# A fused two-block layer on one core: soft attention with the first map's scores two tiles ahead, another queue order on VectorE and ScalarE, and operand splits in three pieces

## The chip, the cores and the metric

One core of a Trainium2 chip runs the whole program in one launch. The metric is the device time in microseconds; lower is better. Of the kernel before, three runs gave 3892.44, 3895.23 and 3902.70 us.

## What is computed

Two transformer-like blocks over 1024 tokens of width 1024 in fp32: a block with a convolution branch, differential attention and a mixture of experts, then a block with four mixers and a feed-forward part. The change touches two attentions with a softmax over all earlier tokens. The first block's is differential: each of 4 heads has two maps of 64 channels, and the second map's weights are taken off the first's:

```python
s = einsum("bqhcd,bkhcd->bhcqk", qi, k) * scale      # c: the two maps
s = where(key_pos <= q_pos, s, -inf)
p = softmax(s, axis=-1)
a = p[:, :, 0] - lam * p[:, :, 1]
return einsum("bhqk,bkhe->bqhe", a, v)
```

The second block's (`_fox`) has 4 heads of 64 channels and a decay added to the scores: `s = q k + c_q - c_k`, masked, softmax, times v.

## The kernel before

`soft_attention` (L663) serves both. The **paired** call (tag `da`, from `first_block`, L2776) works on 4 pairs of maps, one head each; the **unpaired** call (tag `fx`, from `mixers`, L2842) on 2 pairs, two heads each. A *unit* u is a pair i and a tile t of 128 queries: t runs from 0 to 7 (NT = 8), and since attention is causal, a unit has t+1 tiles of 128 keys. x is 0 or 1, the map in the pair. All engines go through the units in one list, each with a queue order of its own, written out by hand; counting semaphores tie them.

**Operands.** fp32 scores come from fp32r matmuls, so q and k are split into a rounded part and a remainder. `round_off` (ScalarE, L782) writes the rounded part: three copies for a map (L785, L786, L789), four in the unpaired call (L788 too). `remainders` (VectorE, L829) writes the differences, two for a map (L833, L834), once `hi_made` says that the copies are there. `lo_made` frees the scores. The split is made in two pieces of columns, 0 to 256 and 256 to 1024, each waited for at t=0 and t=2. There is one buffer for all pairs, so the split of the next pair waits until the last scores of this one are done. In the unpaired call POOL also moves two rows of decay for each map by DMA (L714), and the scores of t=0 wait for both.

**A unit.** `scores` (TensorE, L724) fills two PSUM banks for each map (0 and 1, 2 and 3) by L732 and L733, and L734 adds the mask; it waits for the exponential of the unit before on the same map, which frees the banks. `peaks` (VectorE, L840) takes the row maxima. `exps` (ScalarE, L796) takes exponentials and their sums. `combine` (VectorE, L846 to L851) takes the sums' reciprocals and, in the paired call, adds the second map's weights to the first's by L851. `turn_weights` (TensorE, L747) transposes the weights in chunks of up to four tiles, which alternate between banks 4 and 5: chunk c waits until chunk c-2 has been kept. The paired call turns one map (1 or 2 chunks a unit), the unpaired call two (2 chunks, 4 from t=4 on). `keep_turned` (ScalarE, L806) copies them out of PSUM. `weigh` (TensorE, L759) multiplies by the values, t+1 matmuls for a map, of 128 columns in the paired and 64 in the unpaired call, each with two records in the trace; it has banks 6 and 7. `finish` (VectorE, L858) scales the result.

**Queue order before,** in the iteration of unit u (within a pair):

```python
TensorE: scores(u+1, 0), scores(u+1, 1), turn_weights(u), weigh(u-1)
ScalarE: exps(u+1, 0), keep_turned(u), exps(u+1, 1)
VectorE: peaks(u+1, 0), combine(u), peaks(u+1, 1), finish(u-1)
```

In the iteration of t=7 TensorE issues the next pair's scores behind weighing, ScalarE the first piece ahead of the keeping copy and the second between the exponentials of the next t=0, and VectorE the differences likewise.

Of the kernel before, what the change touches and what calls it, by code (L numbers as in the profile page):

```python
# [662 lines left out]
def soft_attention(K, tag, q_tiles, k_tiles, values, v_col, dv, o, o_col, paired, exps_room, turned_room, decay=None):  # L663
# [7 lines left out]
    pieces = ((0, 2 * P), (2 * P, S))  # L671
# [9 lines left out]
    with ExitStack() as scope, nc.Block() as block:  # L681
# [20 lines left out]

        def exps_of(u, x, n):
            return exps_room[u % 2][x][:, 0:n]

        if decay is not None:
            @block.gpsimd
            def _(pool):
                pool.wait_ge(filled, 1)
                for i in range(pairs):  # L710
                    for x in range(2):
                        if i:
                            pool.wait_ge(scored, 2 * (NT * i - 1) + x + 1)
                        pool.dma_start(k2[(1 - x) * HD:(1 - x) * HD + 2, x, :], decay[2 * i + x]).then_inc(decay_landed, 16)  # L714

        @block.tensor
        def _(pe):
            mm = nc.tensor.matmul

            def scores(u, x):  # L720
                i, t = units[u]
                if t in (0, 2):
                    pe.wait_ge(lo_made, 4 * i + 2 * (t > 0) + x + 1)
                if t == 0 and decay is not None:  # L724
                    pe.wait_ge(decay_landed, 32 * i + 32)
                if u:
                    pe.wait_ge(exped, 2 * (u - 1) + x + 1)
                n, queries = (t + 1) * P, slice(t * P, (t + 1) * P)
                bank = score_bank(x, n)
                for b in range(0, n, HALF):  # L730
                    keys = slice(b, min(b + HALF, n))
                    mm(bank[:, keys], q1[:, x, queries], k1[:, x, keys], start=True, stop=False)  # L732
                    mm(bank[:, keys], q2[:, x, queries], k2[:, x, keys], start=False, stop=(keys.stop < n))  # L733
                mm(bank[:, n - P:n], K.ident_r[:], K.causal_r[:], start=False, stop=True).then_inc(scored, 1)  # L734
# [28 lines left out]
            for x in range(2):  # L763
                scores(0, x)
            for u, (i, t) in enumerate(units):
                ahead = u + 1 if u + 1 < len(units) else None
                if t < NT - 1:
                    scores(ahead, 0)
                    scores(ahead, 1)
                turn_weights(u)  # L770
                if u:
                    weigh(u - 1)
                if t == NT - 1 and ahead:
                    scores(ahead, 0)
                    scores(ahead, 1)
# [3 lines left out]
        def _(act):  # L779
            def round_off(i, piece):  # L780
                cols = slice(*pieces[piece])
                for x in range(2):  # L782
                    if i:
                        act.wait_ge(scored, 2 * (NT * i - 1) + x + 1)
                    nc.scalar.activation(k1[own(x), x, cols], k_tiles[own(x), i, cols], ACT.Copy)  # L785
                    nc.scalar.activation(q1[own(x), x, cols], q_tiles[own(x), i, cols], ACT.Copy)  # L786
                    if decay is not None:
                        nc.scalar.activation(q2[own(x), x, cols], q_tiles[own(x), i, cols], ACT.Copy)  # L788
                    nc.scalar.activation(k1[other(x), x, cols], k_tiles[own(x), i, cols], ACT.Copy).then_inc(hi_made, 1)  # L789
# [19 lines left out]
            for piece in range(2):  # L809
                round_off(0, piece)  # L810
            for x in range(2):
                exps(0, x)
            for u, (i, t) in enumerate(units):
                if t < NT - 1:
                    exps(u + 1, 0)
                    keep_turned(u)
                    exps(u + 1, 1)
                    continue
                if i + 1 < pairs:
                    round_off(i + 1, 0)  # L820
                keep_turned(u)
                if i + 1 < pairs:
                    exps(u + 1, 0)
                    round_off(i + 1, 1)
                    exps(u + 1, 1)

        @block.vector
        def _(dve):
            def remainders(i, piece):  # L829
                cols = slice(*pieces[piece])  # L830
                for x in range(2):
                    dve.wait_ge(hi_made, 4 * i + 2 * piece + x + 1)
                    nc.vector.tensor_tensor(k2[own(x), x, cols], k_tiles[own(x), i, cols], k1[own(x), x, cols].bitcast(F32), ALU.subtract)  # L833
                    nc.vector.tensor_tensor(q1[other(x), x, cols], q_tiles[own(x), i, cols], q1[own(x), x, cols].bitcast(F32),  # L834
                                            ALU.subtract).then_inc(lo_made, 1)
# [35 lines left out]
            for piece in range(2):  # L871
                remainders(0, piece)
            for x in range(2):
                peaks(0, x)
            for u, (i, t) in enumerate(units):
                if t < NT - 1:
                    peaks(u + 1, 0)
                    combine(u)
                    peaks(u + 1, 1)
                    if u:  # L880
                        finish(u - 1)
                    continue
                combine(u)
                if i + 1 < pairs:
                    remainders(i + 1, 0)
                finish(u - 1)
                if i + 1 < pairs:
                    peaks(u + 1, 0)
                    remainders(i + 1, 1)
                    peaks(u + 1, 1)  # L890
# [2021 lines left out]
```

## Time and profile before

| | us |
|---|---|
| median of three runs | 3895.23 |
| the profiled execution, its own time | 3911.31 |
| its span, first to last instruction | 3909.3 |
| mean granted TensorE clock | 0.863 |
| TensorE, VectorE, ScalarE, GpSimd busy | 3215.3, 1489.7, 1110.4, 243.3 |
| paired call | some 374 to 566 |
| unpaired call | some 2205 to 2320 |

All times in the rows are counted from the start of the span. An engine's queue is strictly in order, so an instruction that waits holds up all behind it. "Idle before" is the time in which the engine did nothing ahead of the instruction, with the one that released it. The clock is the share of full speed that TensorE was granted.

### The profile page before, as it was taken

The page shows a single profiled execution, that of the slowest core. Times are in us where ns is not written, and L with a number is a line of the kernel's source. Part 1 is how long each engine was busy: PE and PEld are TensorE (multiplying, and loading weights), DVE is VectorE, ACT ScalarE, POOL GpSimd, SP SyncE. Part 2 cuts the span into 40 slices and gives each one's busy share as a digit, 9 for nine tenths or more (in the row PEclk, how much of TensorE's full clock was granted, in tenths as well). Part 3 has the DMA queues.
Part 4 walks back from the last instruction along what each step waited for, and adds up shares of the span by engine and source line. Part 5 has one row for each costly group of instructions (what it writes and reads, how often), then busy time and mean ns, then how long its engine had stood idle before and what let it go on. Part 6 is the DMA issues. An engine that isn't in the chain of part 4 may idle for free. (4 is left out here: it accounts for less than half of the span.)

```text
span 3909.3 us, 40094 instructions
## 1 busy us (share of the span) xinstructions
PE 3215.3 (82%) x14307; PEld 2421.1 (62%) x14307; DVE 1489.7 (38%) x1914; ACT 1110.4 (28%) x1677; POOL 243.3 (6%) x279
## 2 busy tenths in 40 slices
PE   4994659999389999993999478962796789999998
PEld 3882556667345555552788366741794668888786
DVE  2996561113323333334000422368334443333334
ACT  3123541112233333334121543330011432222232
POOL 0220000000100000001221000100000000000000
PEclk8996889999699999996999775565577989999999
DMA  2115002102389999983211101100000311111122
GB/s 77 38 44 172 1 1 66 47 16 86 115 313 343 335 344 334 341 323 140 59 43 31 60 11 28 27 3 11 12 0 14 121 43 54 43 53 43 39 95 75
DMA packets 267644, 391.13 MB, mean 100 GB/s; under 512 B 34001, under 2 KB 150792, under 8 KB 267560
## 3 DMA queue, kind: packets, MB, share of 16 engines
q1 hardware_dynamic: 246344, 339.06, 25.7%
q0 software_dynamic: 9392, 29.99, 2.3%
q10 hardware_dynamic: 11824, 21.00, 1.4%
q8 instruction: 48, 0.79, 0.1%
q14 instruction: 36, 0.29, 0.0%
HBM read 334.33 MB, written 55.68 MB: 100 GB/s over the span
## 5 line engine op out<-in xcount | busy, mean ns | idle before, releaser
L1743 PE MATMUL banks<-h_hi,u_w_hi 128*128 128x512 f32 x704 | 274.8, 390 | 10.6 <-DVE u_w_lo L1777 10.6
L1744 PE MATMUL banks<-h_lo,u_w_hi 128*128 128x512 f32 x704 | 274.6, 390 | 0.0
L1745 PE MATMUL banks<-h_hi,u_w_lo 128*128 128x512 f32 x704 | 274.4, 390 | 0.0
L1381 PE MATMUL banks<-e_wg,e_xT 128*128 128x512 f32 x512 | 227.6, 598 | 1.2 <-ACT e_xT L1411 1.2
L1381 PE MATMUL banks<-e_wu,e_xT 128*128 128x512 f32 x512 | 224.9, 592 | 0.0
L485 DVE SCALAR_TENSOR_TENSOR conv<-x_first,vectors,conv 128x1024 f32<-128x1024 f32 x120 | 183.8, 1531 | 9.0
L1451 DVE TENSOR_TENSOR e_wd_lo<-e_wd,e_wd_hi 128x1024 fp32r<-128x1024 f32 x128 | 148.2, 1220 | 95.7 <-ACT e_wd_hi L1423 95.7
L1381 PEld LDWEIGHTS banks<-e_wu,e_xT 128*128 128x128 f32 x512 | 97.3, 190 | 122.5 <-issue 122.5
L1381 PEld LDWEIGHTS banks<-e_wg,e_xT 128*128 128x128 f32 x512 | 98.0, 192 | 112.9 <-issue 110.5
L1743 PEld LDWEIGHTS banks<-h_hi,u_w_hi 128*128 128x128 f32 x704 | 132.6, 188 | 38.6 <-issue 11.0
L1423 ACT ACTIVATE e_wd_hi<-e_wd 128x1024 fp32r<-128x1024 f32 x128 | 124.7, 1045 | 110.4 <-DVE e_y L1461 110.2
L1744 PEld LDWEIGHTS banks<-h_lo,u_w_hi 128*128 128x128 f32 x704 | 132.6, 188 | 27.6
L1745 PEld LDWEIGHTS banks<-h_hi,u_w_lo 128*128 128x128 f32 x704 | 132.6, 188 | 27.5
L1597 PE MATMUL banks<-fd_w_hi,fd_s_hi 128*128 128x512 f32 x352 | 138.2, 393 | 8.8 <-DVE fd_s_lo L1656 8.6
L377 PE MATMUL banks<-h_hi,z_w_hi 128*128 128x512 f32 x320 | 127.7, 399 | 12.6 <-POOL z_w_lo L440 12.6
L1598 PE MATMUL banks<-fd_w_lo,fd_s_hi 128*128 128x512 f32 x352 | 137.6, 391 | 0.0
L1599 PE MATMUL banks<-fd_w_hi,fd_s_lo 128*128 128x512 f32 x352 | 137.5, 391 | 0.0
L328 PE MATMUL banks<-consts,n_xn 128*128 128x128 f32 x192 | 43.5, 406 | 104.4 <-ACT n_xn L277 104.3
L378 PE MATMUL banks<-h_lo,z_w_hi 128*128 128x512 f32 x320 | 127.4, 398 | 0.0
L379 PE MATMUL banks<-h_hi,z_w_lo 128*128 128x512 f32 x320 | 127.3, 398 | 0.0
L940 PE MATMUL banks<-h_hi,m_w_hi 128*128 128x512 f32 x256 | 105.2, 411 | 7.4 <-DVE m_w_lo L978 7.4
L1396 PE MATMUL banks<-e_wd_hi,e_midT_hi 128*128 128x512 f32 x256 | 103.1, 403 | 7.0 <-ACT e_midT_hi L1428 7.0
(519 smaller groups left out, 6747.1 us busy)
## 6 DMA issues: line engine op xcount, KB each, us to landing
e_wg<-in_w_gate_e_dram SPq DMA_DIRECT2D x32, 2048.0 KB, 8.9
e_wu<-in_w_up_e_dram SPq DMA_DIRECT2D x32, 2048.0 KB, 16.3
e_wd<-in_w_down_e_dram SPq DMA_DIRECT2D x32, 2048.0 KB, 14.1
yT<-in_ffn_w_up_dram SPq DMA_DIRECT2D x44, 512.0 KB, 3.9
expert_results<-nothing SPq DMA_DIRECT2D x1, 16384.0 KB, 50.1
expert_results<-e_y ACTq DMA_DIRECT2D x32, 512.0 KB, 7.1
fd_w<-in_ffn_w_down_dram SPq DMA_DIRECT2D x44, 256.0 KB, 2.6
z_w<-in_w_in_dram SPq DMA_DIRECT2D x19, 512.0 KB, 3.8
```

Of the source, the lines that this page charges most:

```text
L377: mm(bank, w_hi[:, b, cols], h_hi[:, k, tokens], start=(k == 0), stop=False)
L378: mm(bank, w_hi[:, b, cols], h_lo[:, k, tokens], start=False, stop=False)
L379: last = mm(bank, w_lo[:, b, cols], h_hi[:, k, tokens], start=False, stop=(k == KT - 1))
L485: nc.vector.scalar_tensor_tensor(conv[:, c, :], y[:, c, j:j + S], tap(j), conv[:, c, :], ALU.mult, ALU.add)
L1381: mm = nc.tensor.matmul(bank, xT[:, b, k, :], w[:, b, k, :], start=(k == 0), stop=(k == KT - 1))
L1451: nc.vector.tensor_tensor(wd_lo[:, k, :], wd[:, b, k, :], wd_hi[:, k, :].bitcast(F32), ALU.subtract) \
L1597: nc.tensor.matmul(K.ps[:, t, :], s_hi[:, b, tokens], w_hi[:, b, :], start=first, stop=False)
L1598: nc.tensor.matmul(K.ps[:, t, :], s_hi[:, b, tokens], w_lo[:, b, :], start=False, stop=False)
L1599: mm = nc.tensor.matmul(K.ps[:, t, :], s_lo[:, b, tokens], w_hi[:, b, :], start=False, stop=last)
L1743: nc.tensor.matmul(bank, w_hi[:, up, k, :], h_hi[:, k, tokens], start=(k == 0), stop=False)
L1744: nc.tensor.matmul(bank, w_hi[:, up, k, :], h_lo[:, k, tokens], start=False, stop=False)
L1745: mm = nc.tensor.matmul(bank, w_lo[:, up, k, :], h_hi[:, k, tokens], start=False, stop=(k == KT - 1))
```

## The change

The scores of map 0 go two units ahead, those of map 1 one ahead: `scores(u+2, 0)` stands between turning and weighing, `scores(u+1, 1)` ahead of turning. VectorE has `combine(u)` first, then `peaks(u+1, 1)`, `peaks(u+2, 0)` and `finish(u-1)`. ScalarE has both exponentials of u+1 and then the keeping copy of u. The split is made in three pieces (0 to 256, 256 to 512, 512 to 1024; waited for at t=0, 2 and 4): the first in the iteration of t=6 of the pair before, the second in that of t=7, the third in those of t=0 (map 0) and t=1 (map 1) of the pair itself. No operation is added or removed but for the extra piece. The same order holds in both calls.

```diff
--- before.py
+++ after.py
@@ -668,7 +668,8 @@
     pairs = q_tiles.shape[1]
     units = [(i, t) for i in range(pairs) for t in range(NT)]
     outs = 1 if paired else 2
-    pieces = ((0, 2 * P), (2 * P, S))
+    pieces = ((0, 2 * P), (2 * P, HALF), (HALF, S))
+    starts = {0: 0, 2: 1, 4: 2}
     chunks, last_chunk = [], {}
     for u, (i, t) in enumerate(units):
         for x in range(outs):
@@ -700,6 +701,9 @@
         def out_bank(u):
             return K.ps[:, 6 + u % 2, 0:outs * dv]
 
+        def last_score(i, x):
+            return 2 * (NT * i + NT - 1) + x + 1
+
         def exps_of(u, x, n):
             return exps_room[u % 2][x][:, 0:n]
 
@@ -710,7 +714,7 @@
                 for i in range(pairs):
                     for x in range(2):
                         if i:
-                            pool.wait_ge(scored, 2 * (NT * i - 1) + x + 1)
+                            pool.wait_ge(scored, last_score(i - 1, x))
                         pool.dma_start(k2[(1 - x) * HD:(1 - x) * HD + 2, x, :], decay[2 * i + x]).then_inc(decay_landed, 16)
 
         @block.tensor
@@ -719,8 +723,8 @@
 
             def scores(u, x):
                 i, t = units[u]
-                if t in (0, 2):
-                    pe.wait_ge(lo_made, 4 * i + 2 * (t > 0) + x + 1)
+                if t in starts:
+                    pe.wait_ge(lo_made, 6 * i + 2 * starts[t] + x + 1)
                 if t == 0 and decay is not None:
                     pe.wait_ge(decay_landed, 32 * i + 32)
                 if u:
@@ -760,33 +764,31 @@
                                   start=(j == 0), stop=(j == t))
                 last.then_inc(weighed, 1)
 
-            for x in range(2):
-                scores(0, x)
-            for u, (i, t) in enumerate(units):
-                ahead = u + 1 if u + 1 < len(units) else None
-                if t < NT - 1:
-                    scores(ahead, 0)
-                    scores(ahead, 1)
+            for u, x in ((0, 0), (0, 1), (1, 0)):
+                scores(u, x)
+            for u in range(len(units)):
+                if u + 1 < len(units):
+                    scores(u + 1, 1)
                 turn_weights(u)
+                if u + 2 < len(units):
+                    scores(u + 2, 0)
                 if u:
                     weigh(u - 1)
-                if t == NT - 1 and ahead:
-                    scores(ahead, 0)
-                    scores(ahead, 1)
             weigh(len(units) - 1)
 
         @block.scalar
         def _(act):
-            def round_off(i, piece):
+            def round_off(i, piece, x):
                 cols = slice(*pieces[piece])
-                for x in range(2):
-                    if i:
-                        act.wait_ge(scored, 2 * (NT * i - 1) + x + 1)
-                    nc.scalar.activation(k1[own(x), x, cols], k_tiles[own(x), i, cols], ACT.Copy)
-                    nc.scalar.activation(q1[own(x), x, cols], q_tiles[own(x), i, cols], ACT.Copy)
-                    if decay is not None:
-                        nc.scalar.activation(q2[own(x), x, cols], q_tiles[own(x), i, cols], ACT.Copy)
-                    nc.scalar.activation(k1[other(x), x, cols], k_tiles[own(x), i, cols], ACT.Copy).then_inc(hi_made, 1)
+                if i >= pairs:
+                    return
+                if i and piece == 0:
+                    act.wait_ge(scored, last_score(i - 1, x))
+                nc.scalar.activation(k1[own(x), x, cols], k_tiles[own(x), i, cols], ACT.Copy)
+                nc.scalar.activation(q1[own(x), x, cols], q_tiles[own(x), i, cols], ACT.Copy)
+                if decay is not None:
+                    nc.scalar.activation(q2[own(x), x, cols], q_tiles[own(x), i, cols], ACT.Copy)
+                nc.scalar.activation(k1[other(x), x, cols], k_tiles[own(x), i, cols], ACT.Copy).then_inc(hi_made, 1)
 
             def exps(u, x):
                 i, t = units[u]
@@ -807,32 +809,35 @@
                                          K.ps[:, 4 + c % 2, 0:count * P].rearrange("p (j n) -> p j n", n=P), ACT.Copy).then_inc(kept, 1)
 
             for piece in range(2):
-                round_off(0, piece)
+                for x in range(2):
+                    round_off(0, piece, x)
             for x in range(2):
                 exps(0, x)
             for u, (i, t) in enumerate(units):
-                if t < NT - 1:
-                    exps(u + 1, 0)
-                    keep_turned(u)
-                    exps(u + 1, 1)
-                    continue
-                if i + 1 < pairs:
-                    round_off(i + 1, 0)
+                if t == NT - 2:
+                    round_off(i + 1, 0, 0)
+                if u + 1 < len(units):
+                    for x in range(2):
+                        exps(u + 1, x)
                 keep_turned(u)
-                if i + 1 < pairs:
-                    exps(u + 1, 0)
-                    round_off(i + 1, 1)
-                    exps(u + 1, 1)
+                if t == NT - 2:
+                    round_off(i + 1, 0, 1)
+                if t == NT - 1:
+                    for x in range(2):
+                        round_off(i + 1, 1, x)
+                if t < 2:
+                    round_off(i, 2, t)
 
         @block.vector
         def _(dve):
-            def remainders(i, piece):
+            def remainders(i, piece, x):
                 cols = slice(*pieces[piece])
-                for x in range(2):
-                    dve.wait_ge(hi_made, 4 * i + 2 * piece + x + 1)
-                    nc.vector.tensor_tensor(k2[own(x), x, cols], k_tiles[own(x), i, cols], k1[own(x), x, cols].bitcast(F32), ALU.subtract)
-                    nc.vector.tensor_tensor(q1[other(x), x, cols], q_tiles[own(x), i, cols], q1[own(x), x, cols].bitcast(F32),
-                                            ALU.subtract).then_inc(lo_made, 1)
+                if i >= pairs:
+                    return
+                dve.wait_ge(hi_made, 6 * i + 2 * piece + x + 1)
+                nc.vector.tensor_tensor(k2[own(x), x, cols], k_tiles[own(x), i, cols], k1[own(x), x, cols].bitcast(F32), ALU.subtract)
+                nc.vector.tensor_tensor(q1[other(x), x, cols], q_tiles[own(x), i, cols], q1[own(x), x, cols].bitcast(F32),
+                                        ALU.subtract).then_inc(lo_made, 1)
 
             def peaks(u, x):
                 i, t = units[u]
@@ -869,25 +874,27 @@
             dve.drain()
             dve.sem_inc(filled, 1)
             for piece in range(2):
-                remainders(0, piece)
-            for x in range(2):
-                peaks(0, x)
+                for x in range(2):
+                    remainders(0, piece, x)
+            for u, x in ((0, 0), (0, 1), (1, 0)):
+                peaks(u, x)
             for u, (i, t) in enumerate(units):
-                if t < NT - 1:
-                    peaks(u + 1, 0)
-                    combine(u)
+                combine(u)
+                if t == NT - 2:
+                    remainders(i + 1, 0, 0)
+                if u + 1 < len(units):
                     peaks(u + 1, 1)
-                    if u:
-                        finish(u - 1)
-                    continue
-                combine(u)
-                if i + 1 < pairs:
-                    remainders(i + 1, 0)
-                finish(u - 1)
-                if i + 1 < pairs:
-                    peaks(u + 1, 0)
-                    remainders(i + 1, 1)
-                    peaks(u + 1, 1)
+                if u + 2 < len(units):
+                    peaks(u + 2, 0)
+                if u:
+                    finish(u - 1)
+                if t == NT - 2:
+                    remainders(i + 1, 0, 1)
+                if t == NT - 1:
+                    for x in range(2):
+                        remainders(i + 1, 1, x)
+                if t < 2:
+                    remainders(i, 2, t)
             finish(len(units) - 1)
             dve.drain()
```

## Rows read from the trace of the kernel before

**Rows 1.** The page, part 2: granted TensorE clock in tenths, 40 slices of 97.7 us.
```profile
PEclk8996889999699999996999775565577989999999
```

**Rows 2.** Stretches: us, busy and count per engine, clock, DMA share, GB/s.
```profile
374.00:566.00 192.00, 117.31 (x688) 102.94 (x688) 116.06 (x227) 100.84 (x225) 0.00 (x0) 0.85 0.00 1
...
2205.00:2320.00 115.00, 84.57 (x560) 79.29 (x560) 43.65 (x84) 64.20 (x145) 2.14 (x4) 0.79 0.01 1
...
2254.00:2282.00 28.00, 19.79 (x92) 19.41 (x90) 7.00 (x14) 11.01 (x25) 0.00 (x0) 0.50 0.00 1
...
2284.00:2320.00 36.00, 30.87 (x248) 28.92 (x246) 11.50 (x23) 18.18 (x40) 0.00 (x0) 1.00 0.00 1
```

**Rows 3.** Timeline, paired call, pair 1: start, us, engine, line, operation, tiles, [idle before].
```profile
454.98 1.02 DVE L851 SCALAR_TENSOR_TENSOR da_exps<-da_exps,da_factor 128x768 f32<-128x768 f32 x1
...
456.76 1.28 PE L759 MATMUL banks<-qkv 128*128 128x128 f32 x10
...
459.07 1.23 DVE L840 TENSOR_REDUCE da_low<-banks 128x1 f32<-128x1024 f32 x1 [0.70 <-PE banks L734]
...
460.80 1.15 DVE L851 SCALAR_TENSOR_TENSOR da_exps<-da_exps,da_factor 128x896 f32<-128x896 f32 x1
```

**Rows 4.** Groups by form, paired call: busy us, mean ns, idle before.
```profile
L806 ACT ACTIVATE qkv<-banks 128x512 f32<-128x512 f32 x24 | 14.1, 597 | 23.3 <-PE banks L747 23.2
...
L858 DVE TENSOR_TENSOR qkv<-banks,da_share 128x128 f32<-128x128 f32 x32 | 9.3, 292 | 43.2 <-PE banks L759 43.2
...
L796 ACT ACTIVATE da_exps<-banks,da_low 128x1024 f32<-128x1024 f32 x8 | 8.9, 1115 | 6.9 <-DVE da_low L840 6.9
```

**Rows 5.** Timeline of VectorE, paired call: combinations of pairs 0, 1 and 3.
```profile
412.13 1.15 DVE L851 SCALAR_TENSOR_TENSOR da_exps<-da_exps,da_factor 128x896 f32<-128x896 f32 x1
...
441.71 0.62 DVE L851 SCALAR_TENSOR_TENSOR da_exps<-da_exps,da_factor 128x384 f32<-128x384 f32 x1
...
534.33 0.62 DVE L851 SCALAR_TENSOR_TENSOR da_exps<-da_exps,da_factor 128x384 f32<-128x384 f32 x1
```

**Rows 6.** Groups by form, the unpaired call: copies and differences of the pieces.
```profile
L785 ACT ACTIVATE fx_k<-z_fox_k 64x768 fp32r<-64x768 f32 x4 | 3.4, 838 | 0.1
...
L834 DVE TENSOR_TENSOR fx_q<-z_fox_q,fx_q 64x768 fp32r<-64x768 f32 x4 | 3.8, 953 | 0.1
...
L834 DVE TENSOR_TENSOR fx_q<-z_fox_q,fx_q 64x256 fp32r<-64x256 f32 x4 | 1.7, 419 | 0.1
...
L785 ACT ACTIVATE fx_k<-z_fox_k 64x256 fp32r<-64x256 f32 x4 | 1.7, 414 | 7.9 <-PEq L628 7.9
```

**Rows 7.** Timeline of VectorE, paired call: first pair, combinations of t=0 and t=2.
```profile
386.47 0.35 DVE L851 SCALAR_TENSOR_TENSOR da_exps<-da_exps,da_factor 128x128 f32<-128x128 f32 x1
...
393.05 0.62 DVE L851 SCALAR_TENSOR_TENSOR da_exps<-da_exps,da_factor 128x384 f32<-128x384 f32 x1
```

**Rows 8.** Timeline of TensorE, unpaired call: turning of t=6 behind a keeping copy.
```profile
2246.75 0.95 PE L747 MATMUL banks<-consts,yT 128*128 128x128 f32 x7 [1.32 <-ACT yT L806]
```

**Rows 9.** Timeline of ScalarE, unpaired call: exponentials, map 1, t=1 and t=3.
```profile
2220.34 0.20 ACT L796 ACTIVATION_READ_ACCUMULATOR yT<-banks,fx_low 128x1 f32 x1
...
2226.33 0.22 ACT L796 ACTIVATION_READ_ACCUMULATOR yT<-banks,fx_low 128x1 f32 x1
```

**Rows 10.** Timeline, unpaired call, around the boundary of its two pairs.
```profile
2242.39 0.47 PE L732 MATMUL banks<-fx_k,fx_q 128*128 128x512 f32 x1
...
2247.54 2.79 PE L759 MATMUL banks<-values,yT 128*128 128x64 f32 x24
...
2254.49 6.08 PE L759 MATMUL banks<-values,yT 128*128 128x64 f32 x28
...
2286.15 0.22 ACT L796 ACTIVATION_READ_ACCUMULATOR yT<-banks,fx_low 128x1 f32 x1
```

**Rows 11.** Timeline of TensorE, paired call: turning of t=6, pairs 0 and 1.
```profile
413.34 1.75 PE L747 MATMUL banks<-consts,da_exps 128*128 128x128 f32 x7 [1.95 <-DVE da_exps L851]
...
462.00 0.98 PE L747 MATMUL banks<-consts,da_exps 128*128 128x128 f32 x7 [1.95 <-DVE da_exps L851]
```

## The prediction

> **What bounds the kernel now.** I read the page first: the clock line [rows 1] shows TensorE at half or three quarters of full speed in some slices, two of them where the soft attention runs. The stretch view then gives what the change can touch: the paired call (first block, four pairs) runs some 192 us with TensorE busy 117, VectorE 116 and ScalarE 101; the unpaired one (fox heads, two pairs) 115 us with 85, 44 and 64 [rows 2]. No engine is full in either: what ends last is a ring of hand-overs. 307 us is 7.8% of the span, so a tenth of it would be 0.8% of the kernel.
>
> **The ring of the paired call** is legible in the timeline of one unit [rows 3]. The combination of t=5 starts at 454.98; behind it comes its turning, then weighing of t=4 at 456.76, the scores of t=7 follow, their first maximum starts at 459.07, and VectorE, in order, reaches the combination of t=6 at 460.80: 5.82 us per unit. TensorE waits for VectorE, then VectorE for TensorE.
>
> **Part 1, the order of the long units (t=2 to 6).** Now TensorE issues the scores of map 0 of u+2 between turning and weighing, and VectorE queues the combination ahead of both maxima and the finish behind them. So weighing of u-1 (W) and the maximum of u+2 (R) run side by side, and then comes the finish F. The saving is min(W, R) - F. A maximum over 1024 takes 1.23 [rows 3]; ten records of weighing 1.28 with the pipeline's tail, some 0.11 each; the finish takes 0.29 [rows 4]. With W = 4, 6, 8, 10 records and R 0.82 to 1.23 (the maximum over 1024 scaled, with about 0.15 fixed), the savings are 0.2, 0.4, 0.6 and 0.8 us: 2.0 of the 19.1 us from t=2 to t=6 [rows 3, 5]. Four pairs: -8.0; -0.3 at the end of the last pair, where the keeping copy no longer precedes the exponential. What could be late next is VectorE: combination 1.3 with 0.6 of head, two maxima 2.4 and the finish 0.3 make 4.6 us at t=7, still under 4.9, so the ring stays with TensorE and VectorE together.
>
> **Part 2, the third piece.** A copy of 256 columns takes 0.414 and one of 768 0.838 [rows 6]: 0.83 ns a column and 0.20 fixed, so 512 columns take 0.63; successive starts are closer than durations, so I count 1.2 us for three copies of 256 and 1.8 for three of 512. Differences take 0.419 and 0.953, hence 0.69 at 512, and there are two per map. The kernel's start gets shorter: six ScalarE copies at -0.42 and 0.8 of the differences behind them, -3.3 us in the paired call; with eight copies -4.2 in the unpaired one. But the piece is now made in units t=0 and t=1, at the end of each engine's queue for the unit, in series: exponential of u+1 -> keeping copy -> three copies 1.8 -> two differences 1.4 -> only then the next combination, since VectorE is in order. From the combination of t=0 to that of t=2 took 6.6 us in the first pair [rows 7]; new is 6.6 + 2 x 3.2, less 1.4 for maxima and scores that are ready earlier: 11.6. Start and first pair together: -3.3 + 5.0 = +1.7, and +1.2 for turning and scores at half clock after so idle an opening.
>
> Beside it, the Trainium skill, VectorE: DVE Perf Modes, section on the TRN2 errata, says that small SBUF tiles pay a fixed latency each and advises 512 elements or more. The fitted 0.20 us agrees in kind. It speaks against three pieces: it would charge six (paired) or eight more fixed parts a pair.
>
> **Part 3, the boundaries of the paired call.** From the combination of t=6 (412.13) to t=2 of the last pair (534.33) are 122.2 us; less two stretches of 19.1 that leaves 28.0 us a boundary [rows 5]. New, at full clock: t=6 to t=7 is combination 1.15, differences 0.84, maximum 1.23, exponential 1.2, keeping 1.0, three copies 1.2 (map 1's piece stands behind the keeping copy), differences 0.84, head 0.6 [rows 3, 4, 6]: 8.1. t=7 to t=0 is combination 1.3, maximum and exponential of t=0 0.9, keeping 1.2, six copies 2.4, differences 0.8, head 0.6: 7.2. t=0 to t=2 11.6 as above. Sum 27.0, -1.0 against now. With TensorE at half clock (it is idle some 3.7 us before the scores of the new pair) turning, scores and two weighings add 4.9: 31.9, +3.9. Neither excludes the other; I take 30.6, nearer the cold end, because the clock should come back only partway through this work and TensorE is idle again before t=2: +2.6, three times +7.8. Paired call: -8.3 + 2.9 + 7.8 = **+2.4**, between -8.4 and +7.
>
> **Part 4, the unpaired call.** There four chunks of a unit with t of 4 or more share two banks, and chunk 2 may be turned only once chunk 0 is kept. Today ScalarE keeps it between the two exponentials: TensorE waits 1.32 us at t=6 [rows 8]. Now the keeping copy stands behind the exponential of map 1, which waits for the maximum and the scores. From the start of those scores: 1.05 + maximum 1.23 + exponential 1.2 + copy 0.6 = 4.1 with 0.2 of hand-overs at 4.3; turning of chunks 0 and 1 ends at 1.95; the wait is 2.35, +1.0 us. For t=5 +0.9, for t=4 +0.8: +2.7 in the second pair. In the first the same waits (t=6 counts in the boundary) and some 0.3 of scores come on top of units 0 to 3: from the end of the exponential of t=1 to that of t=3 took 6.0 us [rows 9], and takes 12.0 now; with -4.2 -0.5 at the start this makes +3.2. The two DMAs for the decay rows stand earlier on POOL and TensorE's scores of the new pair wait for both; they are released by scores of t=7 and land about 2.5 us later, under the wait of 2.35 and two turnings, so they cost nothing; without that cover they would cost 2.
>
> The boundary is where it gains: from 2242.39 to the end of the exponential of t=3 at 2286.37 are 44.0 us, and TensorE weighed 28 records in 6.08 us where 24 took 2.79 before [rows 10]: the clock was granted at half, 1.2 GHz, from 2254 to 2282 [rows 2]. The new order spreads that work: hand-walked as above I get 32.6 at full clock and 39.9 at half, so -11.4 or -4.1; that stretch follows waits and weighing of 64 columns as now, so half is three times as likely: -6. With +0.2 for the last units: **+0.1**.
>
> **Part 5, the clock.** Behind a wait of 1.95 us turning seven tiles took 1.75 us once and 0.98 another time [rows 11]: the granted clock fell to 1.2 GHz in one case and not in the other. Part 4 makes six waits of 2.0 to 2.35 us (t=4, 5, 6, twice), longer than nearly all now. A fall costs 24 records x 0.11 = 2.6 and 0.7 of turnings and scores, 3.3 us. Bounds: none (0), all six (+20). I take one and a half: +5.
>
> This is the mechanism of rival B. The Trainium skill, TensorE: Matmul & The Clock Gate, section "A second HAM failure mode: psum-queue depth-cycling", says that short idles between groups that cycle through banks let the clock swing between half and full. It speaks against this change in the unpaired call, and by it the upper bound would hold. By that rule, the trace agrees only in part: waits of 1.3 us left the clock at full.
>
> **Sum.** +2.4 +0.1 +5, about **+7 us**. The profiled execution took 3911.3 us (span 3909.3), 16 above the median of 3895.2; on it the forecast is 3918, on the median **3902**.
>
> **Rivals.**
> A, forecast: gains and losses nearly cancel, -4 to +12 us: 0.55.
> B, the clock decides against it: in the unpaired call it falls behind most waits, five or six times 3.3, and paired boundaries go at half clock: 2.4 + 17 + 4, some +23, 3918. It decides from the fourth fall on. For it: TensorE is busy 19.8 of the 28 us from 2254 to 2282, mostly with weighing of 64 columns, and the clock stayed at half [rows 2, 10]. Against: full clock from 2284 to 2320 now, with waits of 1.3 [rows 2, 8]. Chance 0.22.
> C, faster: the clock stays full over all boundaries. Paired 3 x -1.0 + 2.9 - 8.3 = -8.4; unpaired +6.1 - 11.4 = -5.3 and no falls: -14, 3881. For it: less waiting inside the long paired units. Against: the 3.7 us idle. Chance 0.08.
> D, the third piece weighs more than walked (copies and differences wait on each other in four pieces, not two, at each of six pairs): 1.5 us each more, +16, 3911: 0.15.
>
> What B and D hold over +11.7 gives the slower side; 0.3% is about what a measurement of this kernel can tell from no change. Faster 0.08, same 0.56, slower 0.36. The range takes in A, most of B, and D: 3886 to 3919.
>
> **What would show it.** In the new trace: combinations t=5 to t=6 of the paired call 4.9 us apart instead of 5.8; t=0 to t=2 11 to 14 instead of 6.6 to 9; t=6 to t=7 8.1 instead of 4.6 at boundaries; in the unpaired call waits of 2.0 to 2.4 us before the turning that a keeping copy releases, with durations of the turning beside them telling the clock; first exponentials 3.3 and 4.2 us earlier. The forecast is wrong if units t=0 and 1 stay short (the piece hides), or if the granted clock of the unpaired call leaves 0.7 to 0.9.

## The result and the profile after

The changed kernel is slower. Fifteen runs gave a median of 3926.01 us (3910.84 to 3948.41); fifteen of the kernel before, beside them, gave 3905.83 (3892.44 to 3909.40). The ratio is 1.0056, with a 95% interval of 1.0039 to 1.0072: some 22 us, where +7 had been forecast. The median of 3895.23 on which the forecast was built rested on three runs and lies 10.6 us under that of fifteen. One run of the kernel before, beside the experiments, took 4584.76 us at a mean clock of 0.688, and all ratios leave it out. The profiled execution took 3931.77 us (span 3930.1) against 3911.31, 20.5 more.

The page's clock line, 40 slices of 98.3 us, to be held against [rows 1]: slices 5 and 6 (the paired call) fell from 8, 8 to 7, 7, and slice 23, which holds the first half of the unpaired one, from 7 to 6.
```profile
PEclk8996779999699999996999675555576989999999
```

The stretch view of the two calls after, columns as in [rows 2] (us, busy and count per engine, clock, DMA share, GB/s):
```profile
375.00:569.40 194.40, 127.21 (x688) 113.55 (x688) 117.28 (x242) 104.63 (x249) 0.00 (x0) 0.78 0.00 1
2209.90:2335.00 125.10, 97.44 (x560) 89.51 (x560) 45.11 (x92) 67.95 (x161) 2.15 (x4) 0.74 0.00 1
```
Measured from the first split copy to the last finish, the paired call takes 194.5 us (before 191.2) and the unpaired one 125.0 (before 113.6): +3.3 and +11.4, +14.7 together. TensorE has the same 688 and 560 records in both kernels and yet is busy 10 and 13 us longer than in [rows 2]: the same matmuls ran slower. The stages ahead of, between and behind the calls differ by +0.4, +0.4 and +5.3 us in the two profiled executions, in code that is the same; over all the traces of this study the stage between the calls takes 1640 to 1660 us and that behind them 1579 to 1595 whatever the calls do, so a whole run shows a change of 10 us badly, and the lengths of the calls are the better measure.

The paired ring, one unit of pair 1 in the timeline of VectorE and TensorE (answers to [rows 3]):
```profile
458.05 1.02 DVE L856 SCALAR_TENSOR_TENSOR da_exps<-da_exps,da_factor 128x768 f32<-128x768 f32 x1
...
460.82 1.33 PE L763 MATMUL banks<-qkv 128*128 128x128 f32 x10
461.02 1.23 DVE L845 TENSOR_REDUCE da_low<-banks 128x1 f32<-128x1024 f32 x1 [0.94 <-PE banks L738]
...
462.98 1.15 DVE L856 SCALAR_TENSOR_TENSOR da_exps<-da_exps,da_factor 128x896 f32<-128x896 f32 x1
```
Weighing and the maximum now run side by side, and t=5 to t=6 is 4.93 us instead of 5.82, where 4.9 was forecast. The new order does what it says in this unit. Over the whole stretch from t=2 to t=6 most of the saving is gone again. The stretch view of it, for the first two pairs of the change and the second pair of e4 (an experiment below):
```profile
394.41:413.91 19.50, 16.49 (x86) 14.71 (x86) 12.98 (x24) 10.01 (x23) 0.00 (x0) 0.77 0.00 1
444.33:462.98 18.65, 15.47 (x86) 13.76 (x86) 12.90 (x25) 10.02 (x23) 0.00 (x0) 0.82 0.01 1
...
440.13:456.91 16.78, 12.76 (x86) 11.34 (x86) 12.79 (x24) 10.12 (x25) 0.00 (x0) 1.00 0.01 1
```
Before, this stretch took 19.1 us in each pair at a clock of 1.00; in the change the clock is 0.77 to 0.85 in it.

The unpaired call, timeline of TensorE at t=4, 5 and 6 of its first pair (against [rows 8, 10]) and, behind the sixth line of dots, at t=4 and 6 of its second:
```profile
2241.94 0.73 PE L751 MATMUL banks<-consts,yT 128*128 128x128 f32 x5 [2.08 <-ACT yT L808]
...
2243.45 3.62 PE L763 MATMUL banks<-values,yT 128*128 128x64 f32 x16
...
2251.67 0.85 PE L751 MATMUL banks<-consts,yT 128*128 128x128 f32 x6 [1.61 <-ACT yT L808]
...
2253.34 2.39 PE L763 MATMUL banks<-values,yT 128*128 128x64 f32 x20
...
2260.19 1.59 PE L751 MATMUL banks<-consts,yT 128*128 128x128 f32 x7 [2.65 <-ACT yT L808]
...
2262.11 5.32 PE L763 MATMUL banks<-values,yT 128*128 128x64 f32 x24
...
2303.66 1.95 PE L763 MATMUL banks<-values,yT 128*128 128x64 f32 x16
...
2317.66 1.06 PE L751 MATMUL banks<-consts,yT 128*128 128x128 f32 x7 [2.37 <-ACT yT L808]
2318.51 5.22 PE L763 MATMUL banks<-values,yT 128*128 128x64 f32 x24
```
The six waits for the keeping copy are there: 2.08, 1.61, 2.65, 2.08, 2.24 and 2.37 us. Behind three of them, at t=4 and 6 of the first pair and t=6 of the second, the weighing is slow: 16 records in 3.62 us and 24 in 5.3 and 5.2, where [rows 10] has 24 in 2.79. Behind the other three it is not: 16 records take 1.95 and 20 take 2.39, and one of these waits is 2.08 us like the first. Read in windows of one microsecond, the granted clock falls from 2.4 to 1.2 GHz four times inside the call (near 2243, 2260, 2291 and 2318; before once, at 2253). "Time at half clock" below is what these windows add up to: 64.6 us of the unpaired call (before 47.3) and 85.4 of the paired one (before 58.0).

### The profile page after: what moved, and what is told of

It reads as the page before. It is cut to its first block and busy times, and to the rows that moved or that the text cites. A ratio compares the mean times of both kernels' runs of the same rounds, so it can differ in the third digit from the quotient of the medians.

```text
span 3930.1 us, 40170 instructions
## 1 busy us (share of the span) xinstructions
PE 3242.4 (83%) x14307; PEld 2445.1 (62%) x14307; DVE 1493.1 (38%) x1938; ACT 1117.9 (28%) x1717; POOL 243.9 (6%) x279
## 5 line engine op out<-in xcount | busy, mean ns | idle before, releaser
L1403 PE MATMUL banks<-e_wd_hi,e_midT_hi 128*128 128x512 f32 x256 | 103.1, 403 | 7.0 <-ACT e_midT_hi L1435 7.0
```

## The experiments

The theory after the result: order, waits and copies cost what the sum said, and the clock behind the new waits makes the loss, most of it in the unpaired call. The rivals: the third piece is dearer than walked; the waits themselves cost the time, at any clock; the paired call is to blame. In the table, "calls" are the lengths of the paired and of the unpaired call in the profiled execution, "half" the time at half clock in both, and the ratio is that of the whole kernel to the kernel before, run beside it.

| kernel | ratio, 95% interval | calls, us | half, us |
|---|---|---|---|
| before | 1 | 191.2, 113.6 | 58.0, 47.3 |
| the change | 1.0056 (1.0039 to 1.0072) | 194.5, 125.0 | 85.4, 64.6 |
| e1 new order in the paired call alone | 0.9999 (0.9976 to 1.0021) | 191.0, 113.7 | 75.5, 47.3 |
| e2 in the unpaired call alone | 1.0029 (1.0009 to 1.0049) | 188.3, 125.0 | 54.6, 64.0 |
| e3 unpaired keeping copy between | 0.9984 (0.9964 to 1.0005) | 190.9, 102.9 | 75.2, 32.7 |
| e4 two pieces | 0.9998 (0.9979 to 1.0017) | 183.9, 118.4 | 68.5, 50.7 |
| e5 both of these | 0.9936 (0.9914 to 0.9957) | 184.1, 101.6 | 68.7, 34.3 |
| e6 waits filled | 1.0008 (0.9986 to 1.0031) | 194.6, 113.4 | 85.3, 33.0 |
| e7 two pieces, copy between in both | 0.9921 (0.9891 to 0.9952) | 181.0, 100.9 | 61.4, 33.5 |
| e8 before, unpaired copy last | 1.0038 (1.0009 to 1.0067) | 191.3, 128.2 | 58.0, 68.8 |
| e9 e7, paired boundaries filled | 0.9957 (0.9935 to 0.9980) | 177.5, 100.2 | 44.8, 29.6 |
| e10 three pieces, copy between in both | 0.9981 (0.9966 to 0.9995) | 192.2, 103.1 | 85.3, 32.8 |
| e11 e7 again | 0.9951 (0.9930 to 0.9972) | 180.9, 100.2 | 61.4, 29.6 |

**e1 and e2: which call.** The function stands twice in the file, in the new form and in that of before, and each call takes one of them.
```diff
-        soft_attention(K, "fx", Z["fox_q"][:], ...
+        soft_attention_fx(K, "fx", Z["fox_q"][:], ...   # e1: the form before; e2: only this one is new
```


> The new order in the paired call alone; the unpaired call is as before. Theory C (the loss is the unpaired call: the keeping copy stands behind the exponential of map 1, TensorE waits 2 us or more and its clock falls to half): the paired call lasts some 194 us against 191 before and the whole kernel comes out 2 to 5 us over before. Rival P (the third piece costs about the same per pair in both calls, so four of the six pairs carry two thirds of the loss): 12 to 16 us over before. Rival N (the loss lies outside both calls, in the 5 us that the tail of the trace is longer by): 5 or more over before, with the paired call no longer than 192.

> The new order in the unpaired call alone; the paired call is as before. Theory C: the unpaired call lasts 120 to 130 us against 114, with 2 or more falls of the clock behind waits of 2 us, and the kernel is 12 to 20 us over before. Rival P: 6 to 8 us over before. Rival N: within 5 of before in the call, the rest elsewhere.

Measured: the new order in the paired call alone changes nothing (-0.2 us of the call, ratio 0.9999); in the unpaired one alone it adds 11.4 us to that call and 0.29% to the kernel. By the lengths of the calls the loss is the unpaired call's; by the kernel's intervals e1 lies within -9 to +8 us and e2 at +4 to +19. In e2 the paired call, in its old form, took 188.3 us and not 191.2, with 54.6 us at half clock for 58.0.

**e3: the keeping copy back between the exponentials, in the unpaired call.**
```diff
-                    for x in range(2):
-                        exps(u + 1, x)
+                    exps(u + 1, 0)
                 keep_turned(u)
+                if u + 1 < len(units):
+                    exps(u + 1, 1)
```


> The change, but in the unpaired call ScalarE has the keeping copy between the two exponentials again; all else is new. Theory C: the waits of TensorE before the turning fall from 2.0 to 2.7 us to about 1.3, the clock stays at full in the units with t of 4 to 6, and 6 to 14 us of the 22 come back: 8 to 16 over before is cut to 2 to 10 over before in the whole kernel. Rival P: no more than 2 us come back, as the pieces are untouched. Rival N: nothing comes back.

The unpaired call fell to 102.9 us, 22.1 under the change and 10.7 under before. The stretch view of it, and its turning and weighing of t=6:
```profile
2222.40:2325.30 102.90, 84.19 (x560) 77.25 (x560) 44.91 (x92) 67.72 (x161) 2.15 (x4) 0.84 0.01 1
```
```profile
2264.09 0.95 PE L991 MATMUL banks<-consts,yT 128*128 128x128 f32 x7 [0.45 <-ACT yT L1048]
...
2266.22 2.84 PE L1003 MATMUL banks<-values,yT 128*128 128x64 f32 x24
```
Waits of 0.67, 0.56 and 0.45 us stand where 2.1 to 2.7 stood, and 24 records take 2.84. The waits shortened by 1.1 to 2.2 us each, some 10 us in six; another 12 us went with them, about what e6 below puts down to the clock. Both the waits (expected at 1.3) and the call (expected to give back 6 to 14 us) fell further than expected.

**e4: two pieces, all else as in the change.**
```diff
-    pieces = ((0, 2 * P), (2 * P, HALF), (HALF, S))
+    pieces = ((0, 2 * P), (2 * P, S))
```


> The change with the split in two pieces (0 to 256, 256 to 1024): the second is made in the iteration of t=7, nothing in t=0 and t=1 of a pair. Theory C: each call starts 3 to 4 us later, t=0 to t=2 takes 4 to 6 us less, t=7 to t=0 some 4 us more, so the paired call is within 4 us of the changed one, the waits in the unpaired call stay, and the kernel is 12 to 24 over before. Rival P: the kernel falls to within 6 us of before.

This expectation missed: the paired call came to 183.9 us, 7 to 10 under the change and 7.2 under before, the unpaired one to 118.4, 6.6 under the change. From t=0 to t=2 took 6.4 to 8.7 us (in the change 11.0 to 13.2), t=7 to t=0 11.3 (8.3 to 9.3), t=2 to t=6 16.8 in three pairs and 19.6 in the first (18.4 to 19.5; before 19.1). The waits for the keeping copy stayed, at 2.09 to 2.65 us, and two of the six, those at t=6, were followed by a fall of the clock.

**e5: both edits.**

> Both remedies at once: two pieces in both calls, and in the unpaired call the keeping copy between the exponentials. If the two costs add up: paired call 184 us (as in e4), unpaired 125.0 - 22.1 (e3) - 6.6 (e4) = 96, together 24 less than the 305 of before, the kernel at 0.9935 to 0.995 of before. If both remedies give back the same half-clock time only once: unpaired 101 to 106, the kernel at 0.9955 to 0.9975.

Paired 184.1, unpaired 101.6, ratio 0.9936. The two gains don't add in the unpaired call: 22.1 and 6.6 alone, 23.4 together. That fits the second reading: both take away time at half clock (64.6 us in the change; 32.7, 50.7 and 34.3 in e3, e4 and e5), and it can be taken away once. The kernel's ratio can't tell: its value lies in the range of the first reading, its interval reaches into that of the second.

**e6: is it the wait or the clock?** The change, with 14 matmuls on TensorE that nothing uses in each of the six waits. They write a free score bank, so what the engine waits for comes no earlier.
```diff
+                    if not paired and x == 1 and j0 == 0 and count == 4 and 4 <= units[u][1] < NT - 1:
+                        if u + 1 < len(units):
+                            pe.wait_ge(exped, 2 * (u + 1) + 1)
+                        for _ in range(14):
+                            mm(K.ps[:, 0, 0:P], K.ident_r[:], K.causal_r[:], start=True, stop=True)
                     if c >= 2:
                         pe.wait_ge(kept, c - 1)
```


> The change, and in the unpaired call 14 matmuls that compute nothing used (identity by mask, 128 columns) ahead of the turning that waits for the keeping copy, in units with t of 4 to 6. The waits stay as long, but TensorE is busy for some 1.5 us of each. If the clock is what makes the waits costly (4 falls of 3.3 us in the changed run): no fall behind these waits, turning and weighing at full speed, and the unpaired call at 111 to 117 us against 125, although TensorE has 84 matmuls more. If the waiting itself is the cost: 125 to 127 us.

The timeline of TensorE at t=6 of the first pair and, behind the dots, at the end of the call:
```profile
2251.38 0.93 PE L996 MATMUL banks<-consts,yT 128*128 128x128 f32 x7
2252.06 1.76 PE L992 MATMUL banks<-causal_r,ident_r 128*128 128x128 f32 x14
2254.86 0.99 PE L996 MATMUL banks<-consts,yT 128*128 128x128 f32 x7 [1.04 <-ACT yT L1053]
2255.97 2.84 PE L1008 MATMUL banks<-values,yT 128*128 128x64 f32 x24
...
2307.94 0.99 PE L996 MATMUL banks<-consts,yT 128*128 128x128 f32 x7 [0.76 <-ACT yT L1053]
2308.77 2.79 PE L1008 MATMUL banks<-values,yT 128*128 128x64 f32 x24
```
The two turnings start 3.48 us apart here and 3.58 in the change (2256.61 and 2260.19): the stall is as long as before. But the weighing behind it takes 2.84 instead of 5.32, and the call 113.4 instead of 125.0. Work that does nothing took 11.7 us off. That is the price of the clock, since order, copies and dependences are those of the change; the falls behind the three waits are gone. The clock still falls three times in this call, near 2223, 2261 and 2281, none of them right behind a filled wait; the last is the change's fall at t=2 of the second pair, behind the same idle time of 2.31 us. So the 11.7 us are the price of three falls, 3.9 each. By stretches from second turning to second turning, the change against this run: t=4 to t=5 of the first pair 9.7 and 7.2 us, t=6 to t=4 of the second pair 42.0 and 37.8, and the last t=6 to the end of the call 17.3 and 12.9; that is 2.6, 4.3 and 4.4. The kernel's ratio, 1.0008, says the same as the calls: no slower than before.

**e8: the kernel before, with the unpaired keeping copy last and nothing else.**
```diff
                     exps(u + 1, 0)
-                    keep_turned(u)
                     exps(u + 1, 1)
+                    keep_turned(u)
```


> The kernel before, with one edit: in the unpaired call ScalarE has both exponentials ahead of the keeping copy. Scores, maxima and pieces are as before. Theory: TensorE's wait in front of the turning grows from 1.3 to some 2.2 to 2.6 us in the units with t of 4 to 6, and with falls of the clock behind some of them the call takes 118 to 128 us instead of 113.6. If the loss needs the new order of the scores as well: the call stays within 113 to 116.

+14.6 us in the call and +0.38%, with waits of 2.39, 2.55, 1.85, 2.38, 2.24 and 1.99 and six falls, one of them at the boundary of the pairs, where before has its only one. The call ends just above the expected 118 to 128. One fall, at t=5 of the first pair:
```profile
2261.44 0.85 PE L980 MATMUL banks<-consts,yT 128*128 128x128 f32 x6 [2.55 <-ACT yT L1039]
2262.13 3.26 PE L992 MATMUL banks<-values,yT 128*128 128x64 f32 x20
```
So that one move is enough for a loss of this size without any other part, and the rest of the change gives back some 3 us of it in that call.

**e7, e11: copy between the exponentials in the paired call too, with two pieces,** and **e10: the same with three pieces.** The edit is that of e3 in both calls, with that of e4 in e7 and e11.

> e5 with the keeping copy between the exponentials in the paired call as well. Only one map is turned there, so no turning waits for that copy within a unit; the copy would now delay the exponential of map 1, and so the next combination, by up to 1.1 us where ScalarE is late. Expected: t=5 to t=6 from 4.9 to 5.0 to 5.5 us and the paired call 184 to 190. If the copy's place is of no account in the paired call: 184, and the same time as e5 within 3 us.

> The change with one edit in both calls: ScalarE takes the exponential of map 0, the keeping copy, the exponential of map 1. It keeps three pieces, and so completes the square of pieces and place of the keeping copy. If the third piece costs what it is (copies and differences in the queues of t=0 and t=1), the paired call is 7 to 11 us over that of e7 (181.0), 188 to 192, with t=0 to t=2 at 11 to 13 us; unpaired as e3, 102 to 104; the kernel 0.994 to 0.999 of before. Rival: the third piece hurts only together with the keeping copy at the end, behind which it stands: then the paired call is 181 to 184 and the kernel 0.991 to 0.993.

> The kernel of e7 once more, in five rounds: two pieces, keeping copy between the exponentials in both calls. By the stage lengths it saves 191.2 - 181.0 and 113.6 - 100.9, 22.9 us, 0.9941 of before. Expected 0.992 to 0.996, paired call 180.5 to 181.5, unpaired 100 to 102. If e7's 0.9921 held something of its own, and not scatter of the untouched stages, it comes again at 0.990 to 0.992.

e7 is the best version; its ratio rests on four runs, its repetition gives 0.9951 on ten, and the calls agree within 0.7 us. It is faster than both kernels. That it would cost up to 6 us in the paired call was wrong: t=5 to t=6 stayed at 4.93 us. Of the 3.1 us that the paired call gains on e5, 2.8 lie in t=2 to t=6 of the first pair (19.63 to 16.80), where the clock stayed full; a gain of this size can be the clock's state alone (last section), and the part of the copy's place in it is not shown. e10 closes the square: with the keeping copy in the middle the third piece costs 11.2 us in the paired call (192.2 against 181.0), with the copy last 7.1 to 10.5 (191.0 or 194.5 against 183.9). The rival that the piece hurts only behind a late keeping copy is out.

**e9: fill the paired boundary.** e7, with 24 unused matmuls ahead of the wait for the new map's split.
```diff
+                if i and t == 0 and x == 1:
+                    pe.wait_ge(exped, 2 * (u - 1) + x + 1)
+                    for _ in range(24):
+                        mm(K.ps[:, 2, 0:P], K.ident_r[:], K.causal_r[:], start=True, stop=True)
```


> The e7 kernel (two pieces, keeping copy between the exponentials) with 24 unused matmuls on TensorE in each of the paired call's three boundaries between pairs of heads, ahead of the wait for the new map's split; they compute nothing that is used. Theory one, the half clock behind the boundary's waits costs time there: the turning x8 falls from 1.97 us towards 1.1, the weighing x14 from 3.27 towards 1.8, so t=7 to t=0 falls from about 11.6 us to 9 to 10, the paired call from 181.0 to 174 to 178, and the kernel to 0.990 to 0.992 of before. Rival, the boundary is bound by VectorE's splits and copies and the slow stretch lies beside them: t=7 to t=0 stays within 0.5 us of e7's, the paired call at 180.5 to 182, the kernel at 0.992 to 0.994. If the added matmuls delay the turning instead, the call is 182 to 186.

The timeline of TensorE at the boundary of pairs 1 and 2, first e7, then e9:
```profile
462.37 1.97 PE L751 MATMUL banks<-consts,da_exps 128*128 128x128 f32 x8 [1.36 <-DVE da_exps L855]
...
464.67 3.27 PE L763 MATMUL banks<-qkv 128*128 128x128 f32 x14
...
473.07 0.47 PE L751 MATMUL banks<-consts,da_exps 128*128 128x128 f32 x1 [4.84 <-DVE da_exps L855]
```
```profile
461.80 1.09 PE L755 MATMUL banks<-consts,da_exps 128*128 128x128 f32 x8 [0.74 <-DVE da_exps L859]
...
463.03 1.78 PE L767 MATMUL banks<-qkv 128*128 128x128 f32 x14
...
471.66 0.48 PE L755 MATMUL banks<-consts,da_exps 128*128 128x128 f32 x1 [6.56 <-DVE da_exps L859]
```
Turning and weighing run at full clock, 2.4 us shorter, but t=7 to t=0 shrinks by 0.83 us only, from 11.63 to 10.80, and TensorE's next wait grows from 4.84 to 6.56: there VectorE and ScalarE, with the split of 768 columns, end last. The call gained 3.4 us (177.5); the whole kernel's ratio, 0.9957, shows nothing over e7 (this profile's middle stage took 1657 us). Both theories of this run were half right.

## Why the prediction was wrong, point by point

**The step that failed is Part 5, the clock.** It took one and a half falls at 3.3 us, +5; three of the six waits were followed by a fall at once, and filling the waits takes away 11.7 us, 3.9 a fall. Both the number of falls and the price of one were too low. The mechanism was named with its place and its upper bound (+20 for all six); its number was chosen at the low end, on one pair of equal waits that came out differently [rows 11] and on full clock behind waits of 1.3 us [rows 8]. Waits of 2 us and more had no row of their own in the unpaired call, but the one wait for a keeping copy above 1.32 us that this call had before was followed by its one fall (timeline of TensorE, t=7 of the first pair):
```profile
2252.91 1.78 PE L747 MATMUL banks<-consts,yT 128*128 128x128 f32 x8 [1.71 <-ACT yT L806]
```
It spoke for more falls, and the prediction doesn't weigh it. A fourth fall of the changed call came behind TensorE's idle time of 2.31 us at t=2 of the second pair, and comes with the waits filled too; the waits of 2.08 and 2.24 in that pair left the clock full, and so did 2.09 and 2.24 in both pairs of e4. Which wait makes the clock fall stays open. The forecast's own sign for this part, a clock of the unpaired call outside 0.7 to 0.9, did not show: it was 0.74. The rule of the Trainium skill that the prediction weighed here (TensorE: Matmul & The Clock Gate, "A second HAM failure mode: psum-queue depth-cycling") spoke against the change, and e6 bears it out in kind: three of six, where the forecast had discounted it to one and a half. That it would be all six was the prediction's own reading of the section.

**The same step left a second term at nothing:** half clock inside the long units of the paired call. Part 1 took its saving at full clock, 17.1 us from t=2 to t=6 of each pair. The change took 18.4 to 19.5 there at a clock of 0.77 to 0.85, so four pairs gave -1.0 us and not -8.0; in e4, at full clock, three of the four took 16.8.

**Part 4** had +0.1 for the unpaired call without falls; with the waits filled it came to 113.4 against 113.6, -0.3. The waits were forecast at 2.0 to 2.35 and measured at 1.61 to 2.65. From the end of the exponentials of t=3 to that of t=7 took 25.2 us in the second pair and 22.9 before: +2.2 for a forecast +2.7. From that of t=7 of the first pair to that of t=3 of the second took 36.9 us before, 32.3 after, 28.2 with the waits filled: -4.6 and -8.7, where the boundary was forecast at -6. The filler run itself still had 33.0 us at half clock, so this is agreement of a sum, not of each term.

**Part 1** (-8.3) and **Parts 2 and 3** (+2.9 and +7.8) are parted by e4: the order without the piece gave -7.2 us in the paired call, and the piece on top 7.1 to 10.5 for 10.7. A copy of 512 columns was interpolated at 0.63 us, a difference at 0.69; they took 0.627 and 0.686 us in the mean of eight. t=6 to t=7 was forecast at 8.1 and took 7.96 at each boundary; t=0 to t=2 was forecast at 11 to 14, and took 11.0 to 13.2; the first exponentials come 3.43 and 4.30 us earlier after the start of each call (3.3 and 4.2); a boundary took 29.2 in the mean for 30.6. The paired call was to change by +2.4 and changed by +3.3 in the change and -0.2 in e1. That the sum came near is in part luck. Its terms in the changed run were -1.0 for the long units (forecast -8.0), +0.9 for the start and the first pair (+2.9), and +3.6 for three boundaries (+7.8): savings and costs were both put too high. (With its own terms the prediction's upper end for the call is +6.3, where it says +7, and the stretches of a boundary add up to 26.9, where it says 27.0.)

**The sum.** By the calls the change costs +14.7 us: the forecast's 7.5, with 6.7 more for Part 5, 0.9 more in the paired call and 0.4 less in Part 4. The kernel's ratio says 15 to 28 us. What lies between is not settled: e1 and e2, multiplied, give 1.0028, the two calls of the trace 1.0038, the ratio of the change has 1.0039 at its low end.

**The rivals.** B comes nearest: it was to decide from the fourth fall on, and the call had four, three of them behind the new waits; its sum of +23 was right for the kernel and too high for the calls, since the new waits brought three falls and not five or six, though at 3.9 us each and not 3.3. D (the piece dearer than walked) falls with e4 and e10. C falls; but with the keeping copy where it was and two pieces, the calls do gain 23 us. **The base** was off beside it: +7 on the median of fifteen would have been 3913, still 13 short, and the range, moved by the same 10.6, would have ended at 3930 and held the time. The spread of the kernel before, 3892 to 3929 beside the experiments, could not be seen in three.

## What to carry to other kernels

When a reordering keeps the operations and only lengthens TensorE's waits, price each new wait twice: for its length, and for the matmuls behind it at half clock (here the six waits grew by 0.9 us each in the mean, and the three falls behind them cost 3.9 us each). Put the small copy that frees a PSUM bank ahead of work that waits for a chain of its own: moving it behind one exponential made a stage of 102.9 us 22 us longer (e3), and one of 113.6 us 15 us longer (e8). And where a loss of clock is suspected, fill the waits with unused matmuls: if the stage gets shorter with the waits as long as before, it is the clock.

## What was not expected of the hardware

**One schedule has several times.** The paired call of the change and that of e1 have the same instructions in the same order. At t=2 of the first pair and after it, behind waits that agree within 0.02 us, the timeline of TensorE has, in the change and then in e1:
```profile
395.08 0.90 PE L751 MATMUL banks<-consts,da_exps 128*128 128x128 f32 x3 [2.79 <-DVE da_exps L856]
...
402.27 1.48 PE L763 MATMUL banks<-qkv 128*128 128x128 f32 x6
```
```profile
394.18 0.55 PE L751 MATMUL banks<-consts,da_exps 128*128 128x128 f32 x3 [2.77 <-DVE da_exps L856]
...
399.68 0.88 PE L763 MATMUL banks<-qkv 128*128 128x128 f32 x6
```
In windows of one microsecond, the first stays at 1.2 GHz until near 403; the second is at 2.4 at this turning, at 1.2 for some 3 us behind it, and at 2.4 again from 398. In the end the calls take 194.5 and 191.0 us. e6 and e3, which have that paired call too, took 194.6 and 190.9. The old paired call took 191.2 and, in e2, 188.3. So a difference of up to 3.5 us between such stages says nothing of the schedule. In the first microsecond of the call the clock was still full in the two traces of 194.5 and 194.6 us and at half in those of 191.0 and 190.9. This hints that the clock's state is carried on from the stage before; no run here tests it.

**Narrow matmuls show the clock too.** Sixteen records of 64 columns took 1.90 to 1.95 us at 2.4 GHz (e8, e6) and 3.62 at 1.2 behind the first wait of the change. Where the clock is the same all through such a group, its time can be read beside the clock's own column.
